# Other experts in the extra weight slots, and the gate/up product split by parity and by half

## What is computed

```
def expert_block(args):
    xb, e = args
    hdn = jax.nn.silu(xb @ w_eg[e]) * (xb @ w_eu[e])
    return hdn @ w_ed[e]
...
return jnp.einsum('nkd,nk->nd', y_slots, combine.astype(y_slots.dtype))
```

## Time and profile before

| | |
|---|---|
| median of 3 runs | 1128.43 us (1128.16 to 1130.31) |
| profiled execution, its own time | 1133.17 us |
| its span, first to last instruction | 1131.4 us |
| TensorE busy | 986.7 us, 87% |
| VectorE, ScalarE, GpSimd busy | 381.9, 299.2, 72.8 us |
| share of DMA in the chain that ended last | 18% |
| mean granted TensorE clock | 0.95 |
| bytes moved, mean rate | 319.01 MB, 282 GB/s |

### The profile page before, as it was taken

The page is one execution under the profiler, slowest core; times in us unless marked ns, Lnnn a source line. Parts: engine busy times, 40 slices in busy tenths (PEclk is TensorE's granted clock), DMA queues, the critical chain, the costliest instruction groups (busy, mean ns, idle before and its releaser), DMA issues.

```text
span 1131.4 us, 21794 instructions
## 1 busy us (share of the span) xinstructions
PE 986.7 (87%) x7612; PEld 631.9 (56%) x7613; DVE 381.9 (34%) x1079; ACT 299.2 (26%) x685; POOL 72.8 (6%) x149
## 2 busy tenths in 40 slices
PE   4899999899998989877779999999997999897775
PEld 2567677387764444433356767756785644443333
DVE  1138622222351323322242483131326133232224
ACT  2335555300232111111133455451003311111112
POOL 1112000000200000000001110000010000000000
PEclk9899999989998989999988999898997999999998
DMA  9894224994376789999996333289731398999991
GB/s 383 305 418 150 104 84 125 422 420 172 112 297 266 317 333 423 422 422 421 422 411 205 112 112 113 67 312 420 308 144 37 115 388 335 421 421 422 422 422 71
DMA packets 65420, 319.01 MB, mean 282 GB/s; under 512 B 6050, under 2 KB 27874, under 8 KB 28226
## 3 DMA queue, kind: packets, MB, share of 16 engines
q1 hardware_dynamic: 63408, 315.06, 70.0%
q10 hardware_dynamic: 1810, 2.51, 0.6%
q0 software_dynamic: 128, 0.40, 0.1%
HBM read 315.44 MB, written 2.51 MB: 281 GB/s over the span
## 4 chain that ended last, share of the span: by engine, by line
PE 65%; DMA 18%; DVE 8%; ACT 5%; issue 3%; SPq 1%; ACTq 0%; POOL 0%; DVEq 0%; PEldq 0%; POOLq 0%
PE ps L579 19%; DMA ring<-wstream 18%; PE ps L1020 7%; PE ps L656 7%; PE ps L951 4%; PE ps L1029 4%; PE ps L1010 4%; PE ps L997 4%; PE ps L612 3%; PE ps L1000 2%; PE ps L830 2%; DVE work L1376 1%; PE ps L722 1%; ACT work L1204 1%; DVE top L1375 1%
## 5 line engine op out<-in xcount | busy, mean ns | idle before, releaser
L1020 PE MATMUL ps<-ring,work 128*32 128x512 f32 x912 | 116.1, 624 | 42.4 <-DMA ring<-wstream 41.0
L579 PE MATMUL ps<-h,ring 128*128 128x288 f32 x512 | 134.6, 417 | 0.7 <-ACT work L1134 0.7
L579 PE MATMUL ps<-work,ring 128*128 128x288 f32 x512 | 131.4, 415 | 2.9 <-DVE work L1466 2.9
L656 PE MATMUL ps<-h,ring 128*128 128x288 f32 x416 | 108.0, 421 | 9.0 <-ACT h L1148 6.6
L579 PEld LDWEIGHTS ps<-work,ring 128*128 128x128 f32 x512 | 97.7, 194 | 30.0 <-issue 3.7
L579 PEld LDWEIGHTS ps<-h,ring 128*128 128x128 f32 x512 | 97.2, 195 | 29.8 <-issue 4.1
L1265 ACT ACTIVATE mraw<-ps 128x512 f32<-128x512 f32 x64 | 38.2, 598 | 260.6 <-PE ps L1020 258.4
L656 PEld LDWEIGHTS ps<-h,ring 128*128 128x128 f32 x416 | 81.4, 197 | 33.7 <-issue 11.1
L1615 DVE SCALAR_TENSOR_TENSOR h<-work 128x288 f32<-128x288 f32 x128 | 60.6, 515 | 108.7 <-issue 108.7
L1029 PEld LDWEIGHTS ps<-fold,mraw 128*128 128x128 f32 x512 | 64.3, 197 | 56.2 <-ACT mraw L1265 51.1
L1029 PE MATMUL ps<-fold,mraw 128*128 128x32 f32 x512 | 71.1, 284 | 25.8 <-PE ps L1010 19.0
(11 more groups left out here) (240 smaller groups left out, 989.1 us busy)
## 6 DMA issues: line engine op xcount, KB each, us to landing
ring<-wstream SPq DMA_DIRECT2D x274, 1024.0 KB, 15.0
work<-wstream SPq DMA_DIRECT2D x14, 1024.0 KB, 15.2
work<-pages SPq DMA_DIRECT2D x32, 192.0 KB, 3.2
work<-pages SPq DMA_DIRECT2D x32, 128.0 KB, 2.1
cs<-consts SPq DMA_DIRECT2D x1, 1218.0 KB, 8.5
x<-x_in SPq DMA_DIRECT2D x1, 1152.0 KB, 5.3
out_y<-h ACTq DMA_DIRECT2D x2, 576.0 KB, 2.8
out_vp<-work ACTq DMA_DIRECT2D x2, 256.0 KB, 3.3
```

The costliest lines, as they stand in the source:

```text
L579: last = mm(out, w[:, (k0 + k) * stride:(k0 + k) * stride + 128], rhs(k), start=(k == 0), stop=(k == n - 1))
L656: last = mm(ps[:, 0:T], w[:, t * 1024 + k * 128:t * 1024 + (k + 1) * 128], h[:, k, :], start=(k == 0), stop=(k == KD - 1))
L1020: last = mm(pgu[32 * c:32 * c + 32, :], xs[:, k, :], ws[k // 4][:, c * 512:(c + 1) * 512], start=(k < 4), stop=(k >= 4), skip_group_check= ...
```

## The change

It has two parts.

1. `APART` becomes 63 to 69: the extra slots hold experts 21 and 22 and the first gate/up pair of expert 23. The times at which they are loaded stay. With that the code of experts 1 to 20 is the loop (five rounds of four), and 21 to 31 are written out.
2. The up product works on halves of 256 columns. Chunk k writes its gate half to column group 2(k % 2) and its up half to group 2(k % 2) + 1, each of four chunks. Partitions 0 to 31 and 64 to 95 hold the two partial sums of gate (even and odd k), 32 to 63 and 96 to 127 those of up, in 256 columns. ScalarE copies 256 columns. A second folding matrix `fold_pairs` (128 x 64, two identities of 64 on top of each other) adds even and odd: two matmuls of 64 columns give gate and up beside each other, and the views for silu and the product follow the new layout (`pgt`).

```
-APART = range(RING, RING + EXTRA)
-EARLY, ROUND = 7, RING // 3
-LATE = EARLY + (N_EXP - EARLY) // ROUND * ROUND
+ROUND = RING // 3
+LATE = 1 + 5 * ROUND
+APART = range(3 * LATE, 3 * LATE + EXTRA)
...
-        gu = mraw[:, :]
+        gu = mraw[:, 0:256]
...
+        pgt = pgut[:, 0:4 * BLK].rearrange("p (i h s) -> p h i s", i=2, h=2)
...
-            pe.wait_ge(fold_made, 1)
+            pe.wait_ge(fold_made, 2)
...
+                def up_chunk(k, rows, ws):
+
+                    for half in range(2):
+                        c = 2 * (k % 2) + half
+                        at = (k % 4) * 512 + half * D_EXP
+                        last = mm(pgu[32 * c:32 * c + 32, 0:D_EXP], rows, ws[k // 4][:, at:at + D_EXP],
+                                  start=(k < 2), stop=(k >= KD - 2), skip_group_check=True)
+                    return last
...
                     for k in range(KD):
-                        c = k % 4
-                        last = mm(pgu[32 * c:32 * c + 32, :], xs[:, k, :], ws[k // 4][:, c * 512:(c + 1) * 512],
-                                  start=(k < 4), stop=(k >= 4), skip_group_check=True)
+                        last = up_chunk(k, xs[:, k, :], ws)
...
-                    for i in range(4):
-                        last = mm(pgut[:, i * BLK:(i + 1) * BLK], gu[:, i * 128:(i + 1) * 128], fold[:, :], start=True, stop=True)
+                    for i in range(2):
+                        last = mm(pgt[:, :, i], gu[:, i * 128:(i + 1) * 128], fold_pairs[:, :], start=True, stop=True)
...
-                for e in range(1, EARLY):
-                    expert(e, table[0:1, 1, e + 1:e + 2])
-                with pe.Fori(0, (LATE - EARLY) // ROUND) as er:
+                with pe.Fori(0, (LATE - 1) // ROUND) as er:
                     for j in range(ROUND):
-                        expert(EARLY + j, table[0:1, 1, bass.ds(er * ROUND + EARLY + j + 1, 1)], er)
+                        expert(1 + j, table[0:1, 1, bass.ds(er * ROUND + j + 2, 1)], er)
...
-                        act(gu, pgu[:, :], ACT.Copy).then_inc(gu_kept, 1)
+                        act(gu, pgu[:, 0:D_EXP], ACT.Copy).then_inc(gu_kept, 1)
...
+            V.tensor_tensor(fold_pairs[:, :], ident[:, 0:2 * BLK], ident[:, 2 * BLK:4 * BLK], ALU.add).then_inc(fold_made, 1)
```

More of the change, by code:

```diff
@@ L247, in decoder_trunk @@
         dest = sb("dest", [128, 16, 3])
-        cnt = sb("cnt", [128, 4, N_EXP])
+        cnt = sb("cnt", [128, 3, N_EXP])
+        fold_pairs = sb("fold_pairs", [128, 2 * BLK])
         mraw = sb("mraw", [128, 512])
@@ L958, in _ @@
                         banks.wait_drained(pe, l, f"x{KD - 1}.0")
-                    c = k % 4
-                    last = mm(pgu[32 * c:32 * c + 32, :], xsort[:, k, 0:BLK], ws[k // 4][:, c * 512:(c + 1) * 512],
-                              start=(k < 4), stop=(k >= 4), skip_group_check=True)
+                    last = up_chunk(k, xsort[:, k, 0:BLK], ws)
                 last.then_inc(gu_done, 1)
@@ L1264, in _ @@
                         a.wait_ge(gu_done, n + 2)
-                        act(gu, pgu[:, :], ACT.Copy).then_inc(gu_kept, 1)
+                        act(gu, pgu[:, 0:D_EXP], ACT.Copy).then_inc(gu_kept, 1)
                         a.wait_ge(gut_done, n + 1)
-                        act(sg, pgut[:, 0:2 * BLK].rearrange("p (i s) -> p i s", i=2), ACT.Silu).then_inc(silu_done, 1)
+                        act(sg, pgt[:, 0], ACT.Silu).then_inc(silu_done, 1)
                         a.reg_add(seen, seen, 1)
@@ L1617, in _ @@
                         d.wait_ge(silu_done, n + 1)
-                        V.tensor_tensor(hdn, sg, pgut[:, 2 * BLK:4 * BLK].rearrange("p (i s) -> p i s", i=2), ALU.mult).then_inc(hdn_ready, 1)
+                        V.tensor_tensor(hdn, sg, pgt[:, 1], ALU.mult).then_inc(hdn_ready, 1)
                         d.wait_ge(combined, n + l + 1)
```

## The result

The changed kernel takes 1150.8 us (median of four runs, 1146.1 to 1153.5) against 1128.3 for the kernel before: 1.0201 times as long, 95% interval 1.0169 to 1.0233. Run again beside other kernels it gave 1.0203 (1.0167 to 1.0239). The forecast was 1112 us. The kernel is slower; the mechanism is that of rival D, at a loss that the forecast had priced too low, with some of rival C beside it.

What follows compares the result with a forecast made beforehand. Both expert phases were taken to end DMA-bound, lengthened by DMA standstills. The terms -12.8 - 5.8 - 2.0 - 0.2 + 4.0 gave -16.8 us; 16.4 off the 1128.43 us median made 1112 us, range 1103 to 1124.

Steps and rivals of the forecast that it cites:

- rival D: Written-out experts 21 to 31 stall one by one; slower from 1.7 us lost per expert, 1140 us at 2.2; chance 0.06.
- a loss that the forecast had priced too low: First-time code in written-out experts 21 to 31: 0.77 us lost per expert, mostly absorbed by slack, leaving 2 us a layer.
- rival C: Loop's first round (experts 1 to 4) stalls, starving DMA 3 to 8 us a layer: 1124 to 1130; chance 0.06.

Runs made afterwards that it cites:

- e11: The kernel before, old block, with extra slots moved to written-out experts 17 to 19 between two loops (1 to 16, 20 to 31): 1110.6 us, ratio 0.9833.
- e5: The kernel before with twelve never executed turn matmuls added to the code for further blocks in experts 1 to 31: 1141.3 us, ratio 1.0143.
- e3: The changed kernel with never taken second-block code cut to one register instruction in written-out experts 21 to 31: 1114.7 us, ratio 0.9861 to the kernel before.
- e8: The changed kernel with the ring's expert pairs bringing half their bytes, so outputs aren't the reference's: 1082.8 us, timed once.

## What to carry to other kernels

Before writing a loop's body out, or adding instructions to a body that is written out, count its code like a resource: pieces of 16 KB, here one in 5 to 6.2 us on average where TensorE waited for them, against the time in which the engine works through them, skipped code included. First-time code belongs where the engine waits for something else anyway, and not at the end of a phase; a second loop behind the written-out middle, with the old block, made the kernel 1.7% faster (e11, 0.9833) where the change made it 2% slower. A rate of loss read from one kernel holds for that kernel's ratio of code to work; near a limit it doesn't scale.

## What the runs showed of the hardware

- 12 matmuls per expert that are never executed made a kernel 1.4% slower (e5), and removing never executed code from the written-out experts of another made it 3.3% faster (e3).
- All 81 unexplained waits of 1 us or more in TensorE's expert phases, over thirteen kernels, ended 1.2 to 2.1 us after a 16 KB packet of the instruction queue had come in.
- TensorE's code came in 16 KB packets of about 1 us each, 5.0 us apart on average with the DMA engines 37% busy (e8), 5.7 at 84% (e8) and 6.2 with them nearly full (changed kernel, layer 0). Single distances went from 3.0 to 9.0 us, so 5 to 6 us is a mean and no fixed time of a piece. Halving the expert weights' bytes took back about a third of the lost time.
- A loop of four experts with 76 matmuls of code each was fetched once: between 400 and 495 us, experts 9 to 21 of layer 0 in the changed kernel, the instruction queue moved one packet, at 494 us.

```profile
q8 instruction: 1, 0.02, 0.1%
```
